# Late modulation blocks: 128 of 1024 columns in a ring of two slots, instead of 256 of 512 columns in a ring of four

## The reference

```python
c_act = jax.nn.silu(c)                       # c: (1, 2048)
mod = c_act @ w_ada[layer] + b_ada[layer]    # w_ada: (2048, 6 * 2048)
sh1, sc1, gt1, sh2, sc2, gt2 = jnp.split(mod[:, None, :], N_MOD, axis=-1)
h = rmsnorm(x, g_mix[layer]) * (1 + sc1) + sh1
x = x + (1 + gt1) * mixer(h, positions, w_in[layer], w_a[layer], w_b[layer], w_o[layer])
h = rmsnorm(x, g_ffn[layer]) * (1 + sc2) + sh2
x = x + (1 + gt2) * conv_ffn(h, w_up[layer], conv_w[layer], conv_b[layer], w_down[layer])
```

## Time and profile before

| | |
|---|---|
| median of three timed runs | 3112.95 us (3110.6 to 3118.21) |
| profiled execution, its own time | 3115.91 us |
| its span, first to last instruction | 3114.2 us |
| TensorE busy / VectorE busy / ScalarE busy | 93% / 65% / 43% of the span |
| GpSimd busy | 5%, of which 137.5 us are the issues of L2899 |
| mean DMA rate over the span | 188 GB/s |
| late sums, L2055 | 256 of 689 ns, 166.4 us busy together |
| late blocks, L2899 | 256 of 256 KB, 4.6 us from issue to landing (median) |
| chain that ended last | TensorE 79%, VectorE 11%, DMA 4% |
| of it, landings of late blocks | 2% |

### The profile page before, as it was taken

One profiled execution on the slowest core, in us unless ns is written; L12 is line 12 of the kernel. 1 busy time (PEld: TensorE's weight loads), 2 busy tenths in 40 slices (PEclk: granted clock), 3 DMA queues, 4 the chain that ended last, 5 costly groups with the idle time before them and its releaser, 6 DMA issues.

```text
span 3114.2 us, 61464 instructions
## 1 busy us (share of the span) xinstructions
PE 2898.8 (93%) x24496; PEld 2759.2 (89%) x24496; DVE 2035.4 (65%) x3170; ACT 1343.3 (43%) x1897; POOL 167.2 (5%) x288
## 2 busy tenths in 40 slices
PE   1799999999999999998999999889799999999997
PEld 1789898999988888888999999888789999998997
DVE  7877898777567666664446566664676666665445
ACT  1265334333355555553445444223354444443443
POOL 0111012222000000000000000011000000000000
PEclk7899999999999999999999999999899999999999
DMA  9977578899545555554554555400335555554552
GB/s 389 317 241 246 166 239 267 300 301 305 199 151 188 188 189 189 187 190 151 183 183 147 176 159 163 136 3 4 122 136 176 182 182 189 182 182 162 189 187 96
DMA packets 407683, 586.92 MB, mean 188 GB/s; under 512 B 20416, under 2 KB 368704, under 8 KB 390016
## 3 DMA queue, kind: packets, MB, share of 16 engines
q1 hardware_dynamic: 384864, 517.28, 49.7%
q0 software_dynamic: 20480, 67.13, 6.2%
q10 hardware_dynamic: 2208, 0.66, 0.1%
HBM read 582.91 MB, written 2.10 MB: 188 GB/s over the span
## 4 chain that ended last, share of the span: by engine, by line
PE 79%; DVE 11%; DMA 4%; issue 2%; ACT 2%; SPq 0%; DVEq 0%; POOL 0%; POOLq 0%; ACTq 0%
PE bank L465 17%; PE bank L466 17%; PE bank L467 16%; PE bank L472 15%; PE bank L473 8%; PE bank L1198 3%; DMA late_ring<-w_ada_turned_dram 2%; DVE wlo L399 2%; DVE ring L2018 1%; DVE late_ring L2055 1%; DMA ring<-w_ada_turned_dram 1%; ACT whi L388 1%; PE bank L758 1%; DMA ring<-w_in_dram 1%; DVE mats L2626 1%
## 5 line engine op out<-in xcount | busy, mean ns | idle before, releaser
L399 DVE TENSOR_TENSOR wlo<-ring,whi 128x1024 fp32r<-128x1024 f32 x908 | 1086.5, 1220 | 510.8 <-ACT whi L388 509.2
L388 ACT ACTIVATE whi<-ring 128x1024 fp32r<-128x1024 f32 x908 | 940.1, 1052 | 873.9 <-PE bank L467 577.8
L465 PE MATMUL bank<-hx,whi 128*128 128x256 f32 (+3 forms) x2720 | 782.3, 288 | 32.8 <-DVE wlo L399 25.8
L467 PE MATMUL bank<-hx,wlo 128*128 128x256 f32 (+3 forms) x2720 | 774.4, 285 | 0.0
L466 PE MATMUL bank<-hx,whi 128*128 128x256 f32 (+3 forms) x2720 | 773.8, 284 | 0.0
L472 PE MATMUL bank<-hx,whi 128*128 128x512 f32 x2112 | 741.1, 394 | 1.6 <-DVE wlo L399 1.1
L473 PE MATMUL bank<-hx,wlo 128*128 128x256 f32 x2112 | 594.7, 282 | 0.0
L465 PE MATMUL bank<-xs,whi 128*128 128x256 f32 (+1 forms) x1920 | 542.8, 283 | 42.1 <-DVE xs L458 41.4
L465 PEld LDWEIGHTS bank<-hx,whi 128*128 128x128 f32 x2720 | 516.7, 190 | 46.5 <-DVE wlo L399 23.9
L466 PE MATMUL bank<-xs,whi 128*128 128x256 f32 (+1 forms) x1920 | 543.5, 283 | 0.0
L467 PE MATMUL bank<-xs,wlo 128*128 128x256 f32 (+1 forms) x1920 | 540.4, 281 | 0.0
(11 more groups left out here) (323 smaller groups left out, 2576.5 us busy)
## 6 DMA issues: line engine op xcount, KB each, us to landing
ring<-w_in_dram SPq DMA_DIRECT2D x136, 1024.0 KB, 5.9
ring<-w_up_dram SPq DMA_DIRECT2D x88, 1024.0 KB, 5.1
ring<-w_down_dram SPq DMA_DIRECT2D x88, 1024.0 KB, 4.8
ring<-w_gate_up_dram SPq DMA_DIRECT2D x88, 1024.0 KB, 5.1
late_ring<-w_ada_turned_dram POOLq DMA_DIRECT2D x256, 256.0 KB, 4.6
ring<-w_oab_dram SPq DMA_DIRECT2D x32, 1024.0 KB, 5.6
ring<-w_ada_turned_dram SPq DMA_DIRECT2D x28, 1024.0 KB, 7.5
ring<-w_out_dram SPq DMA_DIRECT2D x16, 1024.0 KB, 5.3
```

Source lines behind the costliest of these rows:

```text
L388: nc.scalar.activation(half_of(whi, u, h, n), ring[:, u % PLAN[phase][3], h * n // 2:(h + 1) * n // 2], ACT.Copy)\
L399: nc.vector.tensor_tensor(half_of(wlo, u, h, n), ring[:, u % PLAN[phase][3], h * n // 2:(h + 1) * n // 2], half_of(whi, u, h, n).bitcast(F ...
L465: nc.tensor.matmul(out_ap, a[0], b[0], start=start, stop=False, **kw)
L467: return nc.tensor.matmul(out_ap, a[1], b[0], start=False, stop=stop, **kw)
```

## The change

`LATE` becomes 1024 and the ring of the late blocks gets a size of its own, two slots (`LSLOTS`), so it still has 8 KB per partition. There are 128 blocks of 512 KB. The loops work on eight blocks at a time (`LPER`), and wherever four small sums stood in VectorE's order, two large ones stand. The first 1024 columns of all 64 rows are summed in the sb, qi and dsa stages, the second 1024 in the merge loop. GpSimd waits with block j for block j - 2. There are two semaphores for landings instead of four, two columns of partial sums instead of four, and two additions less at the end.

```diff
@@
 NSLOT = 4
-LATE = 512
+LATE = 1024
+LSLOTS = 2
+LPER = 8
 NCHUNK = D // LATE
@@
-        late_ring = sb("late_ring", [P, NSLOT, LATE], at=xs_at)
+        late_ring = sb("late_ring", [P, LSLOTS, LATE], at=xs_at)
@@
-            for n in range(2):
-                nc.scalar.activation(c_chunk[n], c_all[:, n * LATE:(n + 1) * LATE], ACT.Copy).then_inc(c_ready, 1)
+            nc.scalar.activation(c_early, c_all[:, 0:LATE], ACT.Copy).then_inc(c_ready, 2)
@@
-                n = j % NSLOT
-                dve.wait_ge(late_landed[n], b * (16 * KD // NSLOT) + 16 * (j // NSLOT + 1))
+                n = j % LSLOTS
+                dve.wait_ge(late_landed[n], b * (16 * LPER // LSLOTS) + 16 * (j // LSLOTS + 1))
@@
-            def late(c, i, j0, j1):
+            def late(stage, i, j0, j1):
 
                 for j in range(j0, j1):
-                    late_sum(i + 4 * c, j, c, c_chunk[c], i * KD + j)
+                    late_sum(i + 4 * stage, j, 0, c_early, i * LPER + (2 * KD * stage + j))
 
             def late_merge(i, j0, j1):
 
                 for j in range(j0, j1):
-                    late_sum(i + 8, j, 2 + j % 2, c_merge[:, j % 2 * LATE:(j % 2 + 1) * LATE], i * 8 + j // 2)
+                    late_sum(i + 8, j, 1, c_merge, i * LPER + j)
@@ (as an example of the places in VectorE's order)
-                late(0, i, 0, 4)
+                late(0, i, 0, 2)
                 rest_unit("sb", 4, i)
@@
-                    late_merge(i, 4 * (u - 2), 4 * (u - 1))
+                    late_merge(i, 2 * (u - 2), 2 * (u - 1))
@@
-            step.mark(nc.vector.tensor_tensor(late_mod, late_sums[:, 0, :], late_sums[:, 1, :], ALU.add))
-            step(nc.vector.tensor_tensor(late_sums[:, 2, :], late_sums[:, 2, :], late_sums[:, 3, :], ALU.add))
-            step(nc.vector.tensor_tensor(late_mod, late_mod, late_sums[:, 2, :], ALU.add))
+            step(nc.vector.tensor_tensor(late_mod, late_sums[:, 0, :], late_sums[:, 1, :], ALU.add))
@@
-            def late_loads(b, row):
-                for j in range(KD):
-                    if not first(b) or j >= NSLOT:
-                        pool.wait_ge(late_used, b * KD + (j + 1 - NSLOT))
-                    f, c = row(j)
+            def late_loads(b, row, c):
+                for j in range(LPER):
+                    if not first(b) or j >= LSLOTS:
+                        pool.wait_ge(late_used, b * LPER + (j + 1 - LSLOTS))
+                    f = row(j)
@@
-            repeat(pool, 4, lambda i: late_loads(i, lambda j: (i * KD + (2 * KD + j), 0)))
-            repeat(pool, 4, lambda i: late_loads(i + 4, lambda j: (i * KD + (2 * KD + j), 1)))
-            repeat(pool, 8, lambda i: late_loads(i + 8, lambda j: (i * 8 + (2 * KD + j // 2), 2 + j % 2)))
+            repeat(pool, 8, lambda i: late_loads(i, lambda j: i * LPER + (2 * KD + j), 0))
+            repeat(pool, 8, lambda i: late_loads(i + 8, lambda j: i * LPER + (2 * KD + j), 1))
```

More of the change, by code:

```diff
@@ L319, in build @@
         ada_used = sem("ada_used")
-        late_landed = [sem(f"late_landed{n}") for n in range(NSLOT)]
+        late_landed = [sem(f"late_landed{n}") for n in range(LSLOTS)]
         late_used = sem("late_used")
@@ L499, in build @@
         small = small[:, 0, :]
-        c_all = work[:, 6 * KW * T - 5 * LATE:6 * KW * T - 5 * LATE + D]
-        c_chunk = [work[:, WORK - 2 * LATE:WORK - LATE], work[:, WORK - LATE:WORK]]
-        c_merge = work[:, 0:2 * LATE]
+        c_all = work[:, 6 * KW * T - D - LATE // 2:6 * KW * T - LATE // 2]
+        c_early = work[:, WORK - LATE:WORK]
+        c_merge = work[:, 0:LATE]
         ada_first = work[:, 0:ADA_FIRST * D].rearrange("p (a n) -> p a n", a=ADA_FIRST)
@@ L2101, in sb @@
                     sb_softplus(i)
-                late(0, i, 4, 8)
+                late(0, i, 2, 4)
                 rest_unit("sb", 5, i)
@@ L2107, in sb @@
                     sb_differences(i)
-                late(0, i, 8, 12)
+                late(0, i, 4, 6)
                 ahead(rest_unit, "sb", i, last)
@@ L2113, in sb @@
                 nc.vector.tensor_copy(vS[:].rearrange("p a t -> p (a t)"), bank[:, 2, :]).then_inc(v_read, 1)
-                late(0, i, 12, KD)
+                late(0, i, 6, LPER)
                 if first(i):
@@ L2134, in _ @@
             sb_masked(4)
-            late(1, 0, 0, 4)
+            late(1, 0, 0, 2)
             dve.wait_ge(sines, 4)
@@ L2161, in _ @@
                 rope_pair(s)
-                late(1, 0, 4 * s + 4, 4 * s + 8)
+                late(1, 0, 2 * s + 2, 2 * s + 4)
             score, other = s_a[:, 0, :], s_a[:, 1, :]
@@ L2238, in dsa @@
                 rest_unit("dsa", 2, i)
-                late(1, i, 0, 4)
+                late(1, i, 0, 2)
                 rest_unit("dsa", 3, i)
@@ L2245, in dsa @@
                 dsa_probs(i)
-                late(1, i, 4, 8)
+                late(1, i, 2, 4)
                 rest_unit("dsa", 5, i)
@@ L2249, in dsa @@
                 rope(kT[:].rearrange("p a t -> p (a t)"), bank[:, 1, :], 2 * T, tabs128, 64, k2_read, i + 1)
-                late(1, i, 8, 12)
+                late(1, i, 4, 6)
                 ahead(rest_unit, "dsa", i, last)
@@ L2254, in dsa @@
                 nc.vector.tensor_copy(vS[:].rearrange("p a t -> p (a t)"), bank[:, 2, :]).then_inc(v2_read, 1)
-                late(1, i, 12, KD)
+                late(1, i, 6, LPER)
                 step.end()
@@ L2890, in _ @@
             pool.wait_ge(phase_done, 3 * 2)
-            def late_loads(b, row):
-                for j in range(KD):
-                    if not first(b) or j >= NSLOT:
-                        pool.wait_ge(late_used, b * KD + (j + 1 - NSLOT))
-                    f, c = row(j)
+            def late_loads(b, row, c):
[3 more added lines that the diff above has]
+                    f = row(j)
                     v = feature_major(A["w_ada_turned"])
                     v = v[:, f:f + 1, :] if isinstance(f, int) else v[:, bass.ds(f, 1), :]
-                    nc.gpsimd.dma_start(late_ring[:, j % NSLOT:j % NSLOT + 1, :], v[:, :, c * LATE:(c + 1) * LATE])\
-                        .then_inc(late_landed[j % NSLOT], 16)
-            repeat(pool, 4, lambda i: late_loads(i, lambda j: (i * KD + (2 * KD + j), 0)))
-            repeat(pool, 4, lambda i: late_loads(i + 4, lambda j: (i * KD + (2 * KD + j), 1)))
-            repeat(pool, 8, lambda i: late_loads(i + 8, lambda j: (i * 8 + (2 * KD + j // 2), 2 + j % 2)))
+                    nc.gpsimd.dma_start(late_ring[:, j % LSLOTS:j % LSLOTS + 1, :], v[:, :, c * LATE:(c + 1) * LATE])\
+                        .then_inc(late_landed[j % LSLOTS], 16)
+            repeat(pool, 8, lambda i: late_loads(i, lambda j: i * LPER + (2 * KD + j), 0))
+            repeat(pool, 8, lambda i: late_loads(i + 8, lambda j: i * LPER + (2 * KD + j), 1))
             pool.wait_ge(consts_in, 16)
```

6 lines of the change are left out of this document (3 added, 3 removed).

## The result

The change makes the kernel slightly slower. The median is 3119.91 us (16 runs, 3111.56 to 3124.22), beside 3112.21 us for 16 runs of the kernel before (3106.92 to 3118.21). The ratio is 1.0023, 95% interval 1.0016 to 1.0031. On 3112 us that is **+7.2 us** (5.0 to 9.6), about half of the forecast +14.5, and inside its range. It is less than the 0.3% that the prediction took as the least that can be told from no change; with this many runs it can be told all the same.

What follows compares the result with a forecast made beforehand. TensorE was taken as the limit almost everywhere up to 788 us, late landings costing only above a threshold. Terms 11.7 + 2.2 + 1 - 0.4 = +14.5 us, from a median of 3112.95 to 3127.5 us, range 3110 to 3141.

Steps and rivals of the forecast that it cites:

- rival D: GpSimd's issue doubles with the block, X = 4.5: +26 us, 3139 us; chance 0.10.
- the threshold: Merge iterations 1 to 7: TensorE stands still for whatever E has above 24.1 us and loses nothing below it.
- X: Growth of E per merge iteration through later refills and doubled landings: taken as 3.0 us.
- E: Time in a merge iteration from the first late-sum group's start to the fourth's end; forecast 3 us longer.
- +11.7 us: Merge iterations 1 to 7: with X = 3.0 E exceeds 24.1 us by 14.8 in all, against 3.1 now.
- hops 1 and 3: First-to-second and third-to-fourth group in a merge iteration: each grows 1.2 us, partly hidden in the queue behind a weight block.
- hop 2: Second to third late-sum group in a merge iteration: grows by 1.2 us; 4.1 us from issue to use.
- G4: Fourth group of late sums in a merge iteration, after unit 5: shortens from 2.7 to 2.5 us.
- Iteration 0: Of the merge loop: the rounding of ybs stands behind two longer hops, +2.2 us (1 to 3).
- the stages before the merge loop: Longer landing waits against shorter sums on the chain: +1 us, between -2 and +3.
- rival B: Late issue and part of the landing vanish behind weight blocks, X 1.5 to 2.0: +5 to +7 us, 3119; chance 0.28.
- C: Not slower: larger pieces land so much better that hops do not grow, -3.8 us, 3109; chance 0.12.

Runs made afterwards that it cites:

- after_again: The changed kernel, not edited, run again for a second trace: ratio 1.0020 (1.0011 to 1.0029) to the kernel before.
- before_again: The kernel before, not edited, run again as a control and for a second trace: 0.9998 (0.9988 to 1.0009).
- early_only: Large blocks in two slots up to the end of the dsa stage, small blocks in four slots in the merge loop: 0.9998 to the kernel before.
- two_loads: The changed kernel with each 1024-column slot filled by two transfers of 256 KB, the sum waiting for both: 1.0037 (1.0024 to 1.0049) to the kernel before.
- three_slots: The changed kernel with a third slot of 1024 columns in the merge loop, in the place of the early c row: 0.9993 to the kernel before.
- g4_later_large: The changed kernel with the last group of late sums moved behind the next unit 0's rest in merge iterations 1 to 7: 0.9997 to the kernel before.
- late_ybs: The last-group move plus, in iteration 0, the ybs rounding ahead of the third group: 1.0007 with small blocks, 1.0011 with large, to the kernel before.
- before_c: The kernel before, not edited, traced once more; its mean E was 22.6 us, no time ratio given.
- after_c: The changed kernel, not edited, traced once more; its mean E was 25.1 us, no time ratio given.
- merge_only: Small blocks up to the end of the dsa stage, large blocks in two slots in the merge loop alone: 1.0027 (+8.4 us) to the kernel before.
- one_ahead: The changed kernel, but each block is issued only when the block before it has been summed: 3432.46 us in its only run, +320.

## Why the prediction was off in size

**What held.** The sums are 128 of 1.22 us, the issues 128 of 0.53 us (no dearer for 512 KB, so rival D is out), the landing waits of iterations 1 to 7 went from 24.8 to 33.2 us in three traces of the kernel before to 48.6 to 51.6 in three of the changed one (forecast some 55, from 33.2), the first refill is 0.54 us later, the threshold stands at 24.1, and the merge loop carries the cost. X, the growth of E, was taken as 3.0. Over the four small traces E is 22.25 on average and over the five large ones 24.99: **X = 2.7**.

**The step that failed: "+11.7 us" for iterations 1 to 7.** It added X to the seven E's of one trace and took off the excess that this trace had. The excess is not linear in E: an iteration pays only when it crosses 24.1, so it matters how far below it the iterations stand. The trace at hand had a mean E of 23.1, and the three others of the small blocks have 22.0, 22.6 and 21.3. The prediction's own sum, made with X = 3.0 on each, gives 11.7, 5.5, 9.4 and 2.6, a mean of 7.3. The mechanism was right, and its input was one sample, the highest of four. The prediction took off its total the 2.96 us by which its profiled execution lay above the median, but left the E's of that execution as they were. TensorE's waits for rounding rests show the same miss: 2.3, 2.8 and 3.7 us in the three traces of the changed kernel, where about 14 were forecast. In place of 11.7 the runs show 6.5 (mean of the five large traces) less 1.55 (of the four small ones), **+5.0 us**; between the traces of one group the excess differs by up to 11 us, so this mean is good to about 2. X = 2.7 on the four small traces would give 5.9. The remaining 0.9 fits the fact that the large blocks' E's lie closer together: 24.1 to 25.6 in after_again, 20.5 to 25.7 in before_again.

**A step wrong in its place.** The prediction held that hops 1 and 3, which queue behind a weight block, could hide a later issue, and hop 2 not. It was the reverse: h1 grew by 1.39 us (6.78 to 8.17), h3 by 1.14 (6.72 to 7.86), and h2 by 0.24 (5.72 to 5.96). Each of the three was priced at 1.2. The two behind weight blocks paid it in full and hop 2 paid a fifth of it. (In iteration 3 of the trace of before SP issues a block 1.1, 3.9 and 1.6 us ahead of the three refills.) Why hop 2 is spared is open; no run took the weight block away. That G4 would shrink by 0.2 did not show (3.04 to 3.00).

**The small terms.** Iteration 0, from the rest of yas to that of ybs, took 31.2 us on average with small blocks (30.3 to 31.7) and 32.2 with large ones (31.9 to 32.4): +1.0, forecast +2.2 (1 to 3). From the first copy of q to the rest of yas (the stages before the merge loop) it is 386.5 us in the five traces with small blocks there and 384.9 in the four with large ones, -1.6 where +1 was forecast, inside -2 to +3 and with a scatter of 6 us; early_only, 0.9998, agrees. The two additions are gone, at 0.22 us each. With 5.0 in place of 11.7, 1.0 of 2.2 and -1.6 of +1 the sum is 5.0 + 1.0 - 1.6 - 0.4 = +4.0, and the timed runs say 7.2 (5.0 to 9.6). The 3 us between them are not placed; the uncertainty of the excess alone would cover most of them. What follows the merge loop is the same code in all of these and takes from 2309.5 to 2318.0 us by the trace, a spread of more than the whole effect; on average it is 3.3 us shorter in the five large traces than in the four small ones, so it does not place them either.

**The rivals.** The time came out as rival B's (+5 to +7, 3119), but not by its mechanism: X is 2.7, not 1.5 to 2.0, and nothing hides behind the weight blocks. C would have needed hops that do not grow; two of the three grew by more than a microsecond. The Trainium skill's "Perfetto Trace Analysis", section "DMA Optimizations", has both a rule that larger pieces raise throughput and one that smaller ones may start sooner. The first was hardly put to the test: its example is of transfers of 2 KB, and here transfers of 256 KB became 512 KB while the packets of GpSimd's queue on the page of the profile stayed nearly the same, 20480 before and 18432 after for 67.1 MB. With the second the trace agrees only where the smaller piece is also released and used by itself: two_loads, which splits the transfer alone, was not faster (1.0037). The formula of "DMA: Bandwidth & Descriptors" in the Trainium skill, section "Anatomy of one DMA — SWDGE (gpsimd) path", gives an estimated 0.60 us for 256 KB more; the medians of the two profiles differ by 0.8 (4.6 and 5.4), and the time for one block is 2 us above that formula in both.

**The best version.** three_slots, 0.9993 (0.9985 to 1.0002), and g4_later_large, 0.9997, are no slower than the kernel before, and neither beats it by more than its interval. Where the large blocks are wanted for their fewer instructions (VectorE 2022.6 us busy, 2035.4 before, GpSimd 97.5 against 167.2), they need one of the two.

## What to carry to other kernels

A ring of the same bytes in half as many slots is not the same ring: its refill starts later and its first piece is ready later. Here two of the three hops from group to group paid for both. Where a wait is absorbed by slack, find the threshold at which it stops being absorbed, but then take the distribution of the lateness from several traces: one trace gave the threshold to 0.1 us and the growth of the excess wrong by more than a factor of two. Work whose data lands late belongs behind the instruction that TensorE waits for, not ahead of it, and that is worth something only once the lateness crosses the threshold and nothing else waits at the new place (late_ybs).

## What the runs showed of the chip

- GpSimd's issue costs the same for 512 KB (0.53 us) as for 256 KB (0.54).
- A transfer issued by GpSimd beside the weight stream lands between 2.9 and 9.3 us after its issue for 256 KB (before_c, merge loop) and between 3.6 and 7.5 for 512 KB (after_c; up to 9.8 in merge_only).
- The same code has a mean E of 22.0, 22.6 and 23.1 us in three executions, and these executions took from 3110.38 to 3117.19 us. That is the same size as the effect of the change.
- With 15.0 us of waits of TensorE for rounding rests between 826 and 884 us (one_ahead), its granted clock is 0.88 from 826 to 870 us and 0.74 in the 13 us behind, where it works again, first at 1.2 GHz (0.50) and from 878 us on at 2.4 (1.00); that stretch takes 12.5 us in place of 10.2.
